# Every second tile of peer_u is transposed by VectorE in an earlier stage and kept in DRAM

## The reference

```
h   = rms(x);  P = h @ w_in  -> q, k, v, B, C, xc        # first projection and conv
x   = x + concat(diff_attention(q, k, v), B * conv3(C * xc)) @ w_out
h   = rms(x)                                             # what PEER reads
q   = h @ w_q;  experts, gates = product-key top 16 per head (8 heads)
act = gelu(sum_d(peer_u[experts] * h)) * gates           # one dot product per chosen expert
x   = x + sum(act * peer_v[experts])
```

## Time and profile before

| | |
|---|---|
| time, median of 3 runs | 3289.0 us (3288.17 to 3293.1) |
| the profiled execution | 3283.34 us, of which its span 3281.7 us |
| busy in the span | PE 93%, DVE 69%, POOL 43%, ACT 31% |
| moved by DMA | 863.39 MB, mean 263 GB/s |
| chain that ended last | PE 58%, DVE 17%, issue 10%, DMA 7% |
| granted TensorE clock, mean | 0.97 |

### The profile page before, as it was taken

The page is one execution under the profiler, slowest core; times in us unless marked ns, Lnnn a source line. Parts: engine busy times, 40 slices in busy tenths (PEclk is TensorE's granted clock), DMA queues, the critical chain, the costliest instruction groups (busy, mean ns, idle before and its releaser), DMA issues.

```text
span 3281.7 us, 43444 instructions
## 1 busy us (share of the span) xinstructions
PE 3043.4 (93%) x15841; PEld 2705.6 (82%) x15841; DVE 2249.0 (69%) x2924; ACT 1033.0 (31%) x1315; POOL 1405.6 (43%) x846
## 2 busy tenths in 40 slices
PE   6999999989789999999999999999889999999996
PEld 5887777768679999999999999989787777777874
DVE  3223555532377777787777777778565888888987
ACT  3122333321223233233233333322223444444442
POOL 1000111100025454544454444465744777777882
PEclk8999999999799999999999999999999999999998
DMA  4322433363248887887888788788789999999997
GB/s 168 102 90 83 133 118 120 115 224 102 79 153 309 299 288 269 301 278 279 293 298 295 275 291 284 273 314 312 225 316 365 372 405 406 402 403 407 396 406 276
DMA packets 303709, 863.39 MB, mean 263 GB/s; under 512 B 58228, under 2 KB 191360, under 8 KB 219072
## 3 DMA queue, kind: packets, MB, share of 16 engines
q0 software_dynamic: 102208, 424.02, 35.7%
q1 hardware_dynamic: 182192, 406.88, 34.3%
q10 hardware_dynamic: 19152, 30.42, 2.5%
HBM read 807.61 MB, written 53.61 MB: 262 GB/s over the span
## 4 chain that ended last, share of the span: by engine, by line
PE 58%; DVE 17%; issue 10%; DMA 7%; ACT 4%; POOL 4%; DVEq 1%; ACTq 0%; SPq 0%; POOLq 0%
PE ps L1396 18%; PE ps L1398 17%; PE ps L1397 17%; DMA gates_of<-gate_grid 5%; DVE x_rows L1284 3%; PE ps L1553 3%; ACT uT_hi L871 2%; DVE u_row L1273 2%; POOL gate_grid L626 2%; DVE uT_lo L1262 2%; DVE x_one L1346 1%; DVE v_lo L1308 1%; PE ps L1390 1%; PE ps L1449 1%; DVE pick L1212 1%
## 5 line engine op out<-in xcount | busy, mean ns | idle before, releaser
L1396 PE MATMUL ps<-hT_hi,uT_hi 128*128 128x384 f32 x2048 | 714.8, 349 | 79.2 <-DVE uT_lo L1262 75.1
L1398 PE MATMUL ps<-h2T_lo,uT_hi 128*128 128x384 f32 x2048 | 694.8, 339 | 0.0
L1397 PE MATMUL ps<-hT_hi,uT_lo 128*128 128x384 f32 x2048 | 694.5, 339 | 0.0
L626 POOL DMA_INDIRECT gate_grid<-gates,grid_cells x256 | 494.1, 1930 | 218.5 <-DVE grid_cells L1245 142.4
L1396 PEld LDWEIGHTS ps<-hT_hi,uT_hi 128*128 128x128 f32 x2048 | 392.4, 192 | 94.3 <-DVE uT_lo L1262 74.6
L1262 DVE TENSOR_TENSOR uT_lo<-ps,uT_hi 128x1024 fp32r<-128x1024 f32 x256 | 312.8, 1222 | 206.7 <-ACT uT_hi L871 193.1
L1396 PE MATMUL ps<-v_hi,a_hi 128*128 128x512 f32 x1024 | 407.3, 398 | 43.3 <-DVE v_lo L1308 42.6
L1397 PE MATMUL ps<-v_hi,a_lo 128*128 128x512 f32 x1024 | 404.9, 395 | 0.0
L1398 PE MATMUL ps<-v_lo,a_hi 128*128 128x512 f32 x1024 | 404.3, 395 | 0.0
L1397 PEld LDWEIGHTS ps<-hT_hi,uT_lo 128*128 128x128 f32 x2048 | 392.8, 192 | 1.4
L1398 PEld LDWEIGHTS ps<-h2T_lo,uT_hi 128*128 128x128 f32 x2048 | 391.5, 191 | 0.0
(11 more groups left out here) (172 smaller groups left out, 4977.3 us busy)
## 6 DMA issues: line engine op xcount, KB each, us to landing
u_tile<-in_peer_u SPq DMA_DIRECT2D x128, 1024.0 KB
v_raw<-in_peer_v SPq DMA_DIRECT2D x128, 1024.0 KB
w_raw<-in_w_in SPq DMA_DIRECT2D x24, 1024.0 KB, 5.1
wc_raw<-in_w_in SPq DMA_DIRECT2D x48, 512.0 KB, 3.9
products_all<-products ACTq DMA_DIRECT2D x128, 192.0 KB
gate_grid<-zeros POOLq DMA_DIRECT2D x16, 1024.0 KB
w_raw<-in_w_out SPq DMA_DIRECT2D x16, 1024.0 KB, 5.0
w_peer<-in_peer_w_q SPq DMA_DIRECT2D x16, 1024.0 KB, 11.4
```

The costliest lines, as they stand in the source:

```text
L626: pool.indirect_dma_start(out=gate_grid, out_offset=bass.IndirectOffsetOnAxis(ap=grid_cells[:, d, col:col + 1], axis=0), in_=gates[:, 2 + ...
L1396: mm(out, a_hi, b_hi, start=first, stop=False)
L1397: mm(out, a_lo, b_hi, start=False, stop=False)
L1398: return mm(out, a_hi, b_lo, start=False, stop=last)
```

## The change

Of the 128 tiles of `peer_u`, the odd ones (64) are no longer transposed by PE in the sweep. DVE transposes them while the stages 1 to 3 run. DVE can turn only blocks of 32 × 32, so a tile is loaded such that its four column quarters lie on the four groups of 32 partitions (`load_segments`: 4 DMAs of 256 KB, each to 32 partitions). Four instructions turn it (`turn_segments`), and 8 DMAs of 128 KB, each from 32 partitions, store it to the DRAM tensor `uT_all` (`keep_turned`). There is one `seg_rows` buffer and one pair of `seg_turned` buffers, so a turn waits for its own load and for all stores of the turn before. 24 tiles are turned in the first projection (one behind each weight split), 25 around the attention heads (three in each head), and 15 in the second projection.

In the sweep the even tiles go as before. An odd tile is loaded from `uT_all` into `u_tile[1]`, and ACT and DVE split it straight from there (`uT_rows`) instead of from PSUM. Two pairs of semaphores are merged to make room (`head_mean`, `head_rstd`), and some scratch buffers of the PEER stage now share memory with the segments.

The core of the diff:

```diff
+TURNED = TILES // 2
+QUAD = 32
+QUADS = P // QUAD
+SEGMENT = D // QUADS
...
+TURNS = (1, 2, 4)
...
+        seg_rows = nc.alloc_sbuf_tensor_at("seg_rows", [P, QUADS, SEGMENT], F32, offset=late)
+        seg_turned = [nc.alloc_sbuf_tensor_at(f"seg_turned{i}", [P, 2, SEGMENT], F32, offset=late + (8 + 4 * i) * KB)
+                      for i in range(2)]
...
+        uT_all = nc.dram_tensor("uT_all", (TURNED * P, D), F32, kind="Internal").ap()
...
+        uT_rows = [u_tile[1][:, i * D // 2:(i + 1) * D // 2].rearrange("p (k e) -> p k e", e=P) for i in range(2)]
...
+            def load_segments(n):
+                rows = u_table[bass.ds((2 * n + 1) * P, P), :].rearrange("(g i) (a m) -> a i g m", g=QUADS, a=QUADS)
+                for a in range(QUADS):
+                    sp.dma_start(seg_rows[QUAD * a:QUAD * (a + 1), :, :], rows[a]).then_inc(seg_in, 16)
+            def keep_turned(n, last=False):
+                rows = uT_all[bass.ds(n * P, P), :].rearrange("(b j) (a m) -> a j b m", j=QUAD, a=QUADS)
+                for half in range(2):
+                    sp.wait_ge(seg_ready, 4 * n + 2 * half + 2)
+                    for a in range(QUADS):
+                        sp.dma_start(rows[a][:, 2 * half:2 * half + 2, :],
+                                     seg_turned[half][QUAD * a:QUAD * (a + 1), :, :]).then_inc(seg_stored, 16)
+                if not last:
+                    load_segments(n + 1)
+            def load_weights(chunks, weights, before, turned, order=range(4)):
                 with sp.Fori(0, chunks - 1) as c:
                     for q in range(4):
                         sp.wait_ge(w_ready, 4 * (c + before) + q + 1)
                         load_quarter(weights, c if q < 2 else c + 1, (q + 2) % 4, order)
+                        keep_turned(turned + 4 * c + q)
                 for q in range(2):
                     sp.wait_ge(w_ready, 4 * (before + chunks - 1) + q + 1)
                     load_quarter(weights, chunks - 1, q + 2, order)
+                    keep_turned(turned + 4 * (chunks - 1) + q)
             load_quarter(w_in_v, 0, 0, range(4))
             load_quarter(w_in_v, 0, 1, range(4))
-            load_weights(QKV_CHUNKS, w_in_v, 0)
+            load_segments(0)
+            load_weights(QKV_CHUNKS, w_in_v, 0, 0)
...
+            def keep_by_head(j, p):
+                if p in TURNS:
+                    keep_turned(4 * QKV_CHUNKS + 3 * j + TURNS.index(p))
             with sp.Fori(0, CT - 1) as j:
                 for p in range(PIECES):
                     sp.wait_ge(wc_ready, PIECES * j + p + 1)
                     conv_piece(j + (p + 2) // PIECES, (p + 2) % PIECES)
+                    keep_by_head(j, p)
...
             sp.wait_ge(av_done[1], 2 * HEADS)
             load_quarter(w_out_v, 0, 0, MIX_ORDER)
+            keep_turned(4 * QKV_CHUNKS + 3 * HEADS)
...
-            load_weights(OUT_CHUNKS, w_out_v, QKV_CHUNKS, MIX_ORDER)
+            load_weights(OUT_CHUNKS, w_out_v, QKV_CHUNKS, TURNED - 4 * OUT_CHUNKS + 1, MIX_ORDER)
+            keep_turned(TURNED - 1, last=True)
...
-                    sp.wait_ge(uT_half1_ps[b % 2], TOPK // 2 * i + b // 2)
-                    sp.dma_start(u_tile[b % 2][:, :], u_table[bass.ds(i * TOPK * P + b * P, P), :])\
-                        .then_inc(u_tile_in[b % 2], 16)
+                    if b % 2 == 0:
+                        sp.wait_ge(uT_half1_ps, TOPK // 2 * i + b // 2)
+                        sp.dma_start(u_tile[0][:, :], u_table[bass.ds(i * TOPK * P + b * P, P), :])\
+                            .then_inc(u_tile_in[0], 16)
+                    else:
+                        sp.wait_ge(uT_ready[1], TOPK * i + b - 1)
+                        sp.dma_start(u_tile[1][:, :], uT_all[bass.ds(i * TOPK // 2 * P + b // 2 * P, P), :])\
+                            .then_inc(u_tile_in[1], 16)
...
                 if half == 0:
-                    act.wait_ge(uT_half0_ps, TOPK * i + b + 1)
-                else:
-                    act.wait_ge(uT_half1_ps[b % 2], TOPK // 2 * i + b // 2 + 1)
-                nc.scalar.activation(uT_hi[half][:, :, :], ps_uT[half], ACT.Copy).then_inc(uT_hi_ready[half], 1)
+                    act.wait_ge(uT_half0_next, TOPK * i + b + 1)
+                    if b % 2 == 1:
+                        act.wait_ge(u_tile_in[1], 16 * (TOPK // 2 * i + b // 2 + 1))
+                elif b % 2 == 0:
+                    act.wait_ge(uT_half1_ps, TOPK // 2 * i + b // 2 + 1)
+                nc.scalar.activation(uT_hi[half][:, :, :], ps_uT[half] if b % 2 == 0 else uT_rows[half], ACT.Copy)\
+                    .then_inc(uT_hi_ready[half], 1)
...
+            def turn_segments(n):
+                dve.wait_ge(seg_in, 16 * QUADS * (n + 1))
+                if not (isinstance(n, int) and n == 0):
+                    dve.wait_ge(seg_stored, 32 * QUADS * n)
+                for b in range(QUADS):
+                    v.transpose(seg_turned[b // 2][:, b % 2, :].rearrange("p (c g i) -> p c g i", g=QUADS, i=QUAD),
+                                seg_rows[:, :, :].rearrange("p g (c b j) -> p b c g j", b=QUADS, j=QUAD)[:, b, :, :, :])\
+                                        .then_inc(seg_ready, 1)
             chunks = QKV_CHUNKS
             split_wi(0, 0)
+            turn_segments(0)
             split_wi(0, 1)
+            turn_segments(1)
...
             with dve.Fori(0, chunks - 1) as c:
                 split_wi(c, 2)
+                turn_segments(4 * c + 2)
                 split_wi(c, 3)
+                turn_segments(4 * c + 3)
                 split_wi(c + 1, 0)
                 keep_qkv(c)
+                turn_segments(4 * c + 4)
                 split_wi(c + 1, 1)
+                turn_segments(4 * c + 5)
             split_wi(chunks - 1, 2)
+            turn_segments(4 * chunks - 2)
...
+                v.tensor_scalar(qk_ss[:, :], qk_ss[:, :], 1.0 / HD, EPS, ALU.mult, ALU.add).then_inc(head_mean, 1)
+                turn_segments(3 * j + (4 * QKV_CHUNKS + 1))
+                dve.wait_ge(head_rstd, 2 * j + 1)
                 for i in range(2):
...
                 combined(0)
+                turn_segments(3 * j + (4 * QKV_CHUNKS + 2))
                 biased(2)
...
                 if not last:
                     split_wc(j + 1, 1)
+                turn_segments(3 * j + (4 * QKV_CHUNKS + 3))
...
             split_mix(1)
             split_mix(3)
+            first = TURNED - 4 * OUT_CHUNKS + 1
+            turn_segments(first)
+            turn_segments(first + 1)
             for t in range(TB):
                 dve.wait_ge(x_in[t], 32)
             with dve.Fori(0, chunks - 1) as c:
                 split_wo(c, 2)
+                turn_segments(4 * c + (first + 2))
                 split_wo(c, 3)
+                turn_segments(4 * c + (first + 3))
                 split_wo(c + 1, 0)
                 add_mixed(c)
+                turn_segments(4 * c + (first + 4))
                 split_wo(c + 1, 1)
+                turn_segments(4 * c + (first + 5))
             split_wo(chunks - 1, 2)
+            turn_segments(TURNED - 1)
...
-            def split_u(c, half):
+            def split_u(c, half, by_pe):
                 dve.wait_ge(uT_hi_ready[half], c + 1)
-                v.tensor_tensor(uT_lo[half][:, :, :], ps_uT[half], uT_hi[half][:, :, :].bitcast(F32), ALU.subtract)\
+                v.tensor_tensor(uT_lo[half][:, :, :], ps_uT[half] if by_pe else uT_rows[half], uT_hi[half][:, :, :].bitcast(F32), ALU.subtract)\
                     .then_inc(uT_ready[half], 1)
...
-            def turned(buffer, use, half):
+            def turned(use, half):
                 if half == 0:
-                    pe.wait_ge(u_tile_in[buffer], 16 * use)
+                    pe.wait_ge(u_tile_in[0], 16 * use)
                 for k in range(8):
-                    last = turn(ps_uT[half][:, k, :], u_tile[buffer][:, (8 * half + k) * P:(8 * half + k + 1) * P],
-                                ident[:, :])
-                last.then_inc(uT_half0_ps if half == 0 else uT_half1_ps[buffer], 1)
+                    last = turn(ps_uT[half][:, k, :], u_tile[0][:, (8 * half + k) * P:(8 * half + k + 1) * P], ident[:, :])
+                last.then_inc(uT_half0_next if half == 0 else uT_half1_ps, 1)
             def sweep(i, querying, last=False):
                 for b in range(TOPK):
                     c = TOPK * i + b
                     more = not (last and b == TOPK - 1)
-                    nxt = (b + 1) % 2
                     for half in range(2):
                         pe.wait_ge(uT_ready[half], c + 1)
                         if half == 0:
...
                                                     half == 0 and k == 0, half == 1 and k == 7)
                         if half == 1:
                             summed.then_inc(swept[b % 2], 1)
-                        if more:
-                            turned(nxt, TOPK // 2 * i + (b + 1) // 2 + 1, half)
+                        if more and b % 2 == 1:
```

(3 more changed lines are left out.)

84 lines of the change are left out of this document (50 added, 34 removed).

## The result

The changed kernel runs in 3437.5 us (median of 4), the kernel before beside it in 3288.6: ratio 1.045, 95% interval 1.042 to 1.048. I had forecast 3345 (3245 to 3400), so the time lies above the range. The direction came as written, and so did the wait that was to cause it: DVE in front of its transposes. The size did not, and in the heads and at the start of the second projection waits came that I had not reckoned with.

What follows compares the result with a forecast made beforehand. The prediction took PE to bound the first projection, and PE alternating with a DVE-ACT chain nearly as long to bound the sweep. Terms −47 + 39 + 24 + 40 = +56 us gave 3345 us, range 3245 to 3400.

Steps and rivals of the forecast that it cites:

- Rate on 32 partitions: Turn DMAs: 256 KB on 32 partitions take 1.2 us of transfer, half of the full rate.
- Period 13.0 us: From one turn to the next: 13.0 us, set by transfers of stores, loads and one weight quarter.
- 12.5 for the chain: One turn in series: first two transposes 1.2, stores 4.8, loads 4.8, fixed part 1.7, together 12.5 us.
- First projection 39 us: First projection: 22 periods lose 2.1 us each, 46 us, less a lead of 6.7: 39 us lost.
- the lead of 6.7 us: First projection: a weight split on DVE is 6.7 us ahead of PE, taken off the loss.
- Heads 24 us: Attention heads: turn 2 makes `biased(2)` 3.5 us late, PE fills part; 3 us × 8 = 24 us lost.
- Second projection 40 us: Second projection: one split comes 12 to 13 us late, 13 more quarters lose 2.1 each, 27; 40 us lost.
- Transposes 0.6 us, covered: DVE transposes: 0.6 us each, 2.4 for a turn, covered by DVE's idle time in projections and heads.
- Sweep −47 us: Sweep: six rounds gain 41 us at 188 us each, round 7 nothing, the last round 6; together 47 us gained.
- PE's 113 us: Sweep: 1024 transposes taken from PE, 128 groups of 0.88 us; expected not to come whole.
- the 8.5 us of waits: Sweep, round 4: DVE waits for PE eight times, 8.5 us together, so a round cannot go below 186.4 us.
- The rival with fast small DMAs: Turn DMAs: 256 KB on 32 partitions take 0.6 us, period 10.9 us, total 3255 us; chance 0.30.

Runs made afterwards that it cites:

- narrow4: The changed kernel with 4 stores of 256 KB a turn instead of 8 of 128 KB, still on 32 partitions each: 3482 us (1.059).
- loads_first: The changed kernel with the four loads of the next segment issued before the last four stores of a turn: 3379 us (1.028).
- transposes_only: The changed kernel with all 256 DVE transposes but without the turns' DMAs; odd tiles are read from u_table, their turning left out: 3265 us (0.993).
- before_half: The kernel before, with the sweep's product with u_row on 1024 of 2048 columns: 3246 us (0.987).
- sweep_half: The changed kernel without turns, odd tiles read unturned from u_table, and the product with u_row on 1024 of 2048 columns: 3183 us (0.967).
- plain_both: The changed kernel with loads and 4 stores of 256 KB a turn on all 128 partitions, block arrangement left out: 3294 us (1.0017).
- wide_loads: The changed kernel with a segment's four loads cut by row group, each writing 128 partitions, DRAM pattern beginning with a dimension of 4: 3852 us (1.173).

## Why the prediction was wrong, by its steps

- **Rate on 32 partitions: about right.** I took 1.2 us for 256 KB; 4.5 us per MB came out, 1.1 for 256 KB (1.0 to 1.2 over the three kernels). By the 189 GB/s of the Trainium skill (SBUF — State Buffer, section Door 1: The DMA port swizzle) 1 MB would be 5.5 us, an estimate; here 4.5 us are 233 GB/s, so the direction agrees and the cost is smaller.
- **Period 13.0 us: mis-sized, 13.7.** I had two sums, 12.5 for the chain and 13.0 for the transfers, and took the longer as if it alone counted. The turn shown above goes round in 1.5 + 3.9 + 0.2 + 1.9 + 5.65 = 13.1 us, and the mean of all is 13.7. Issue was quicker than my 0.62 for each DMA (about 0.5), but 5.65 us pass after the last issue. It fits that the last load shares the engines with its three neighbours and with the 1 MB of weights issued right behind; how much of the 5.65 is transfer was not taken apart. That order and start shift the period at equal bytes is shown (`narrow4` +1.3, `loads_first` −1.1).
- **First projection 39 us: 69.** This is the step that failed by its form: where I stopped counting. I counted 22 periods, to the last split of weights, and took the lead of 6.7 us off. But the first head stands on DVE behind turns 23 and 24 (starts 358.63 and 372.05; `sq` at 376.76). 24 periods × 2.8 = 67, and no lead. With my own 13.0 it would have been 51.
- **Heads 24 us: 42 in seven, so 48.** I followed one wait, that of turn 2; it is there, 3.0 to 5.4 us. Missing were the pieces of `wc_raw`, which land after 7.9 us instead of 3.9 and stop ACT ten times, and that they stand behind the turns' stores and loads in SyncE's queue; I had counted them as bytes only. Missing was the lower clock too: I gave it a thought in the sweep alone.
- **Second projection 40 us: 54.** The split that I expected 12 to 13 us late, at 696.14 in the kernel before, stands here:

```profile
829.62 2.49 DVE L1084 STREAM_TRANSPOSE seg_turned<-seg_rows 128x512 f32<-128x512 f32 x4 [16.91 <-DMA seg_rows<-in_peer_u]
832.04 2.25 DVE L1058 TENSOR_TENSOR wo_lo<-w_raw,w_hi 128x2048 fp32r<-128x2048 f32 x1
```

  Counted from the last head's start it comes 98.9 us later (832.04 − 733.1) and not 74.8 (696.14 − 621.3); less 6 for the last head it is 18 us late. The turn in front of it came not one period of 13 but 19.4 us after the one before (at 810.23). From there to the first product of DVE it is 302.4 us against 266.9: 35.5 and not 27, that is 13 quarters × 2.7 and not 13 × 2.1.
- **Transposes 0.6 us, covered: right.** 0.62 each (2.49 for four), and `transposes_only` shows that they are covered, in the heads to within 4.5 us.
- **Sweep −47 us: −23.** That PE's 113 us would not come was right, and `before_half` with `sweep_half` show why. The size was not: round 4 went from 194.9 to 191.0, not 188. Two small terms. What I put at nothing, the odd tile read from SBUF, costs: ACT's rounding takes 42 ns more, and DVE waits 1.29 us instead of 1.19, so 0.8 in a round; round 7, which PE does not bound, is longer (178.6 to 180.4). And of the 8.5 us of waits about 4 stayed in a round where I left 1.6; one of the eight, 0.6 us for ACT's rounding of query weights, was never a wait that PE's time could shorten. The last round gave 3 and not 6.

ACT in the changed kernel's sweep, over the length of one round (1543.5 to 1734.6 us), by source of the tile:

```profile
L936 ACT ACTIVATE uT_hi<-u_tile 128x1024 fp32r<-128x1024 f32 x16 | 17.0, 1060 | 4.4 <-ACT products L957 4.4
L936 ACT ACTIVATE uT_hi<-ps 128x1024 fp32r<-128x1024 f32 x16 | 16.3, 1018 | 5.0 <-PE ps L1650 3.2 <-ACT products L957 1.9
```

Together 30 + 24 + 14 + 24 + 8 (the rest) = 100 us between my +56 and the 156.7 of the two profiled executions. Every term that was off erred to the same side. The rival with fast small DMAs stood on rows of DMAs over 128 partitions only; `plain_both` is about what it would have looked like, 3294 and not 3255: its sweep gave 31 us and not 47, and the stages ahead of it cost 4 + 19 + 15 = 38 us and not 13.

## What to carry to other kernels

Work moved into an engine's idle time brings its DMAs along: add up the ring (compute, stores, loads, landing beside the other transfers) and not only the bytes, and count each period until the consumer that stands behind it, not until the last producer. In one in-order queue a store that waits for compute delays each weight load behind it, so ask of every DMA what is queued after it. And where two engines are nearly as long as each other, relieving one of them pays little: 64 tiles gave 23 us in the sweep instead of 113, and 18 gave 22.

## What I had not expected of the hardware

- How many of the 16 DMA engines a DMA uses depends on the shape of its pattern: with a leading dimension of 4 the share was 0.26 and the rate 102 GB/s, and so the same 256 KB in pieces of the same 2 KB were slower over 128 partitions (`wide_loads`) than over 32.
- 1 MB through 32 partitions at a time occupied the engines 4.5 us (4.0 to 4.8 by the order and number of the DMAs) against 3.2 through 128, with the same pieces of 2 KB.
- In the seven heads PE was busy for 314.5 us at a mean granted clock of 0.94, and for 293.6 us at 1.00, with the same matmuls.
- A 128x1024 rounding on ACT takes 1060 ns from SBUF and 1018 from PSUM.
